# Moving the on-chip buffers of a two-block decoder kernel: a padding buffer removed, a gate buffer and a hidden buffer given places of their own

## What is computed

```
y = sum over picked experts e of  gate_e * gelu(x . u_e) * v_e
...
h = h + concat(y_conv, y_nsa) @ w_out
h = h + memory_attention(rmsnorm(h), rmsnorm(mem), ...)
h = h + peer(rmsnorm(h), ...)
return rmsnorm(h, final_norm_g)
```

## The kernel before

| buffer | place | remainder by 2048 | remainder by 128 |
|---|---|---|---|
| XH, XL, RAW, WH, WL (fixed) | 32896 to 114816 | 128 | 0 |
| start of the arena: HH, YH, SQ | 123008 | 128 | 0 |
| HL, YL, ZX to AA, M, MH, ML, UV0 | further on | 128 | 0 |
| UC (windows of the 31 taps) | 155776 | 128 | 0 |
| YC | 164448 | 608 | 96 |
| T2, QZR0 | 207872 | 1024 | 0 |
| QP (product-key queries) | 147168 | 1760 | 96 |
| QZ0 and SQ2 (first block's attention) | 204928, 209024 | 128 | 0 |
| STG0 (staged gates) | 149216 | 1760 | 96 |
| WGH, GM0 | 134272, 140416 | 1152 | 0 |
| HT | 224640 | 1408 | 0 |

## Time and profile before

### The profile page before, as it was taken

The page is one execution under the profiler, slowest core; times in us unless marked ns, Lnnn a source line. Parts: engine busy times, 40 slices in busy tenths (PEclk is TensorE's granted clock), DMA queues, the critical chain, the costliest instruction groups (busy, mean ns, idle before and its releaser), DMA issues.

```text
span 5241.3 us, 63748 instructions
## 1 busy us (share of the span) xinstructions
PE 4668.8 (89%) x22355; PEld 3896.3 (74%) x22355; DVE 2731.7 (52%) x4130; ACT 1878.7 (36%) x2605; POOL 513.2 (10%) x561
## 2 busy tenths in 40 slices
PE   7998898989999989988899896887765699999999
PEld 6886776768878867766688685676554699999998
DVE  3325456443233254564432385433498766666666
ACT  3424333334234235333343222223216744444444
POOL 0000000000000000000000000000086422222221
PEclk9999999999999999999999986788888999999999
DMA  2221210212222222201222220021111477777776
GB/s 111 96 96 73 81 56 32 72 72 96 96 74 98 93 80 81 73 32 49 73 96 96 74 89 17 0 81 56 56 41 72 190 275 274 278 276 275 274 277 244
DMA packets 85133, 599.75 MB, mean 114 GB/s; under 512 B 10592, under 2 KB 10976, under 8 KB 17952
## 3 DMA queue, kind: packets, MB, share of 16 engines
q1 hardware_dynamic: 57024, 410.85, 21.7%
q0 software_dynamic: 27136, 162.28, 8.8%
q10 hardware_dynamic: 864, 25.17, 1.1%
HBM read 570.99 MB, written 27.26 MB: 114 GB/s over the span
## 4 chain that ended last, share of the span: by engine, by line
PE 74%; DVE 11%; ACT 5%; issue 4%; DVEq 3%; ACTq 1%; POOLq 1%; DMA 1%; POOL 0%; SPq 0%
PE PB L178 21%; PE PB L180 21%; PE PB L179 21%; DVE RS L966 2%; PE PB L687 2%; PE PB L219 2%; DVE WL L164 1%; PE PB L676 1%; ACT STG L2043 1%; PE PB L1659 1%; PE PB L876 1%; ACT WH L158 1%; DVE NM L707 1%; DVEq L255 1%; DVE PB L242 1%
## 5 line engine op out<-in xcount | busy, mean ns | idle before, releaser
L178 PE MATMUL PB<-XH,WH 128*128 128x512 f32 (+2 forms) x3616 | 1379.2, 381 | 185.3 <-DVE WL L164 106.8
L179 PE MATMUL PB<-XL,WH 128*128 128x512 f32 (+2 forms) x3616 | 1364.8, 377 | 0.0
L180 PE MATMUL PB<-XH,WL 128*128 128x512 f32 (+2 forms) x3616 | 1364.4, 377 | 0.0
L164 DVE TENSOR_TENSOR WL<-RAW,WH 128x2048 fp32r<-128x2048 f32 x260 | 606.4, 2332 | 800.0 <-ACT WH L158 794.5
L178 PEld LDWEIGHTS PB<-XH,WH 128*128 128x128 f32 x3616 | 693.6, 192 | 317.0 <-issue 141.6
L179 PEld LDWEIGHTS PB<-XL,WH 128*128 128x128 f32 x3616 | 693.2, 192 | 108.9 <-issue 3.4
L180 PEld LDWEIGHTS PB<-XH,WL 128*128 128x128 f32 x3616 | 691.6, 191 | 103.9
L158 ACT ACTIVATE WH<-RAW 128x2048 fp32r<-128x2048 f32 x260 | 496.8, 1911 | 634.7 <-PE PB L180 593.7
L178 PE MATMUL PB<-WH,WGH 128*128 128x512 f32 x768 | 299.8, 390 | 9.8 <-DVE WGL L2182 9.8
L180 PE MATMUL PB<-WH,WGL 128*128 128x512 f32 x768 | 302.2, 394 | 0.0
L179 PE MATMUL PB<-WL,WGH 128*128 128x512 f32 x768 | 302.1, 393 | 0.0
(11 more groups left out here) (352 smaller groups left out, 7462.8 us busy)
## 6 DMA issues: line engine op xcount, KB each, us to landing
RAW<-weights SPq DMA_DIRECT2D x387, 1024.0 KB, 4.8
gate_matrix<-STG ACTq DMA_DIRECT2D x6, 4096.0 KB, 11.6
GM<-gate_matrix POOLq DMA_DIRECT2D x128, 192.0 KB, 5.3
X<-x SPq DMA_DIRECT2D x1, 2048.0 KB, 8.1
UV<-rows,IDX POOLq DMA_INDIRECT x128, 5.7
out<-FIN SPq DMA_DIRECT2D x4, 512.0 KB, 2.6
MEMX<-mem POOLq DMA_DIRECT2D x1, 1024.0 KB, 5.1
SK<-sub_keys POOLq DMA_DIRECT2D x1, 1024.0 KB, 5.1
```

Of the source, the lines that this page charges most:

```text
L164: c.nc.vector.tensor_tensor(c.WL[p][:, :], c.RAW[p][:, :], c.WH[p][:, :].bitcast(F32), ALU.subtract).then_inc(c.sem("w_split"), 1)
L178: c.nc.tensor.matmul(out, wh, xh, start=start, stop=False)
L179: c.nc.tensor.matmul(out, wh, xl, start=False, stop=False)
L180: return c.nc.tensor.matmul(out, wl, xh, start=False, stop=stop)
```

## The change

Three buffers are placed otherwise:

- ALIGN is gone, so the arena starts 1344 bytes lower, at 121664.
- SG becomes a buffer of its own, of 8192 bytes behind AA.
- HT is declared ahead of BC, in the longer-lived block. It takes 2048 bytes there, so what follows it in that block (BC, HDN, KC, VC, T2, SGB, KVC, QZR to SUM2) lies 704 bytes higher than before, and what precedes it 1344 bytes lower.

```diff
     c.NM, c.SUM = c.sb("NM", [P, 2]), c.sb("SUM", [P, 8])
-    c.sb("ALIGN", [P, 336])
...
             c.ZX, c.XR, c.LG, c.AA = (c.sb(n, [P, DC, S], F32, s) for n in ("ZX", "XR", "LG", "AA"))
-            c.SG = c.AA[:, 0:4, :]
+            c.SG = c.sb("SG", [P, 4, S], F32, s)
...
-            c.BC = c.sb("BC", [P, 2, 2], F32, q)
+            c.HT, c.BC = c.sb("HT", [P, 2, 2, P], F32, q), c.sb("BC", [P, 2, 2], F32, q)
...
                 c.KVC = c.sb("KVC", [P, 2, KV_PAD], F32, r)
-                c.HT = c.sb("HT", [P, 2, 2, P], F32, r)
```

## The result

| | median | range | runs |
|---|---|---|---|
| before | 5245.01 us | 5242.79 to 5246.06 | 6 |
| changed | 5272.61 us | 5271.07 to 5279.77 | 6 |

The ratio is 1.0056, with a 95% interval of 1.0043 to 1.0069: slower, by 27.6 us between the medians. The prediction was 5244.9 us, in a range of 5236 to 5256, with 0.82 on no change. It was wrong. The time and the place that rival B named came (it had 0.08 and 5275 us); the mechanism that it gave did not.

The account below looks back on a forecast made before the run. The prediction took the pace of TensorE's matmuls to bound the kernel. Every term was taken as 0, the sum 0 on 5243.14 us leaving the median at 5244.9 us, in a range of 5236 to 5256.

Parts of the forecast that it names:

- rival B: Main matmuls: streamed operands off a 128-byte place cost up to 5 ns on 6048 matmuls, 30 us, 5275 us; chance 0.08.
- What bounds the kernel: Whole kernel: how fast matmuls follow each other sets the time; TensorE busy 89% of the span, 74% of the chain.
- the first term of the sum: Matmuls on moved buffers in the hot stages: 0 per matmul, bounds -8 and +30 us over 6048 matmuls.
- The witness: Line 1399, streaming YC (remainder 96 by 128) and T2 (0): shortest 593 and 592 ns, taken as place costing nothing.
- The equal pace of the earlier trace: 40 us windows: 178 matmuls with HH streaming, 179 with XH, about 0.225 us each, cited for no change.
- The sign that the prediction had named for it: Changed profile: a median above 390 ns for matmuls on HH but not on XH.
- Its count of 6048: Hot-stage matmuls touching a moved buffer, of 22355: streaming HH, HL, YH, YL, MH, ML, or with WGH, WGL in the array.
- The other terms: VectorE, ScalarE, gate matrix, SG, HT and transfers: 0 each; bounds VectorE 4 us, transfers 1.6 either way, gate -3 and +2.
- Rival C: Gate matrix, line 2043: another base might break the scattered write's 438 ns, 42 us faster, 5203 us; chance 0.03.
- Rival D: Whole span: granted clock falls otherwise, 5232 or 5258 us; chance 0.03 faster and 0.03 slower.
- D's sign: Changed profile: another mean granted clock than 0.943, with unchanged durations.
- Rival E: Whole change: places end up as before, so it doesn't reach the chip; only partly possible, ends at 5244.9 us; no chance given.

Follow-up runs that it names:

- e4: The kernel before with 64 bytes put ahead of X, so every buffer, fixed or in the arena, lies 64 bytes higher: 5243.68 us, ratio 1.0001.
- e9: The kernel before with 368 floats of padding instead of 336, so the arena starts 128 bytes higher: 5282.88 us, ratio 1.0071.
- e6: The kernel before with WH and WL alone 64 bytes higher and the padding 64 bytes shorter, XH and arena unmoved: 5298.61 us, ratio 1.0095.

## Why the prediction was wrong

**What bounds the kernel** held: time moved with TensorE's pace, and the window with HH was the right place to look.

**The step that failed** is the first term of the sum, "I take 0 per matmul" for the moved streamed operands. Its measured value is 6.6 ns on 3744 matmuls, and 13.7 of these microseconds can be read in the down projections. It failed in three ways.

- *The witness couldn't testify.* Line 1399's YC and T2 stood at remainders 96 and 0 by 128, and I compared the streamed places alone. The distance from the standing table of ones (116192) is 128 for YC and 32 for T2, by 256; line 868's is 160. By the measure found later, none of the three is 0, so the pair compared one misplaced case with another; what distance does to the float32 form isn't shown. I also compared the shortest single durations, 592 and 593 ns, of a float32 form that takes about 429 ns from start to start for 512 columns. The form at issue takes 227. A loss of 7 ns on the fast form need not show in one nearly twice as slow.
- *The equal pace of the earlier trace rows was read as evidence.* All streamed operands in it had distance 0 from WH and WL, as the layout table says. An equality among equals says nothing of the new place. The text noted this for the earlier trace rows and then gave the unseen case 0.08.
- *The bound was worked out and left out of the range.* The term's own bounds were -8 and +30 us. The range took 3 us on top for it, with the reason that the mechanism had no row. A missing row is a reason for the whole 30: 5244.9 + 30 would have held the 5272.6. The range also says that it adds to the repeat spread, but its lower end of 5236 is 5244.9 less the 8.6 us of the terms alone.

**Rival B** had the place (HH, YH, MH against XH), the direction and the sum, 5275 against 5272.6, but not the rule. The sign that the prediction had named for it is what came: line 178 in the median at 398 ns on HH and at 389 on XH. Its count of 6048 included the 2304 matmuls with WGH, which lost nothing, and its 5 ns were 6.6; the two errors cancel in part (30.2 us against 24.7), and that its sum came so near is luck. Its mechanism, reads in pieces of 128 bytes from the streamed operand's place, is refuted: e4 has all streamed operands at 64 and is fast, e9 has them at 0 by 128 and is slow.

The rule in the Trainium skill that bears on this (TensorE: Matmul & The Clock Gate, Step-by-step: what each phase is for) says that TensorE has two independent read ports, so that loading the next weights takes nothing from the running matmul's reads. I didn't weigh it. In these runs, with nothing changed but how the two operands lie to each other, the pace went from 226.7 to 233.3 ns. So a streaming matmul's pace does depend here on where the standing operands lie; whether a port, the memory behind it or something else is what they meet isn't shown.

**The other terms** came out as costed. VectorE's taps stood at 750 ns, SG at 685, the scattered write at 1034, UV's landing at 5.7 us (5.4 to 7.7), the mean clock at 0.943. Rival C's write didn't move. Rival D came in part, beside B: the clock fell at other moments in the first down projection (1.6 us), the memory attention (2 us) and the gate stage (2.5 us), while its mean stayed at 0.943, which the prediction had made D's sign. Rival E's end didn't come.

**What stays open.** Why the distance counts, and why in this order (0, 64, 112, 16, 128, 32 = 192 = 224, 240). Why a pair at 112 and 240 paces like 0. Why the experts' first groups are slower than 680 at distance 0. Why 384 columns lose nothing and 256 columns are faster at 64 than at 0. Each would need more distances with clean pairs, at each width; these weren't tried.

## What to carry to other kernels

In float32 matmuls split into high and low parts, at 512 columns, lay the buffer that streams and the buffer that stands a multiple of 256 bytes apart, modulo the steps inside them. This is shown for streamed activations at 512 columns and the full clock alone: at 384 columns nothing was lost, at 256 a distance of 64 was the faster one, and in the expert stage 64 was no worse than 0. Removing a dead buffer, or adding a small one, moves all that is allocated behind it, so compare the matmul pace in a steady window after any change of layout. A row that shows "no effect of place" counts only if it contains both the good and the bad case of the thing that might matter, here a pair of places and not one.

## What was not expected of the hardware

- The pace of these 512-column matmuls at full clock depends on the distance between their two operands in memory, by 256 bytes: 226.7 ns each at 0, 228.9 at 64, 233.3 at 32, 192 and 224, 235.8 at 240.
- The dependence isn't symmetric: 64 costs 2.2 ns and 192 costs 6.6.
- It needs no other engine's instructions. Of the HH matmuls of the changed kernel, those with VectorE, ScalarE and GpSimd all idle have the same mean start to start as the rest, 233.3 ns. The loads of weights by DMA went on meanwhile.
- It depends on the width and the clock. At 384 columns a distance of 192 costs nothing, at 256 columns a distance of 64 is 2% faster than 0, and at 1.2 GHz a group of three takes 1280 ns at 0, 128, 192 and 224.
- What VectorE and ScalarE did here doesn't show it. The taps of line 1544 read at any multiple of 4 bytes in 746 to 758 ns in both kernels. With WH 64 bytes further from RAW (e6), ScalarE's rounding (line 158) stays at 1914 ns and VectorE's difference (line 164) at 2292.
